# Two of four value products of a head as three rounded products, with the scaling of the probabilities moved to GpSimd

## What is computed

```python
def prompt_latent_attention(q_lat, q_pe, ckv, kpe):
    ...
    def block(args):
        ql_b, qp_b, i = args
        sc = (jnp.einsum('bqhc,bkc->bhqk', ql_b, ckv)
              + jnp.einsum('bqhr,bkr->bhqk', qp_b, kpe)).astype(jnp.float32) * SOFTMAX_SCALE
        sc = jnp.where(kpos[None, :] <= qpos[:, None], sc, -jnp.inf)
        p = jax.nn.softmax(sc, axis=-1).astype(ckv.dtype)
        return jnp.einsum('bhqk,bkc->bqhc', p, ckv)

def mla_output(o_lat, z, w_kv_up, w_out):
    o = jnp.einsum('bthc,chv->bthv', o_lat, w_kv_up[..., QK_NOPE_DIM:]).reshape(b, t, D_ATTN)
    return (o * jax.nn.silu(z)) @ w_out
```

## Time and profile before

| | |
|---|---|
| median of 3 runs | 2006.69 us (2005.28 to 2007.47) |
| the profiled execution | 2006.08 us, of which the span of its instructions 2004.4 us |
| TensorE busy | 1945.2 us, 97% of the span |
| VectorE, ScalarE, GpSimd busy | 1415.9 us (71%), 848.7 us (42%), 171.9 us (9%) |
| second group of heads | 1454.7 to 1519.3 us, 64.6 us |
| its end, from the first product of `scores(1)` on | 1492.87 to 1519.3 us |

### The profile page before, as it was taken

The page is one execution under the profiler, slowest core; times in us unless marked ns, Lnnn a source line. Parts: engine busy times, 40 slices in busy tenths (PEclk is TensorE's granted clock), DMA queues, the critical chain, the costliest instruction groups (busy, mean ns, idle before and its releaser), DMA issues.

```text
span 2004.4 us, 42248 instructions
## 1 busy us (share of the span) xinstructions
PE 1945.2 (97%) x16142; PEld 1831.3 (91%) x16142; DVE 1415.9 (71%) x2073; ACT 848.7 (42%) x1318; POOL 171.9 (9%) x124
## 2 busy tenths in 40 slices
PE   4999999999999999999999999999999999999997
PEld 3899999999999999999999999999888887779996
DVE  5597777777777777798778996667433456669776
ACT  3243333333333333364455644446543444455443
POOL 1200000000000000000000250003221122200002
PEclk9999999999999999999999999999999999999998
DMA  9976555555555556654554434448422239852447
GB/s 392 405 268 215 201 196 194 194 194 194 196 203 203 198 203 205 223 190 150 157 181 171 160 131 140 136 134 314 134 72 84 84 104 348 289 184 97 138 149 285
DMA packets 134902, 386.69 MB, mean 193 GB/s; under 512 B 13906, under 2 KB 44498, under 8 KB 131858
## 3 DMA queue, kind: packets, MB, share of 16 engines
q1 hardware_dynamic: 129682, 368.52, 53.2%
q0 software_dynamic: 5120, 16.78, 2.7%
HBM read 353.92 MB, written 31.33 MB: 192 GB/s over the span
## 4 chain that ended last, share of the span: by engine, by line
PE 81%; DVE 8%; DMA 6%; issue 2%; ACT 1%; SPq 1%; DVEq 0%; ACTq 0%
PE ps L965 36%; PE ps L969 18%; DMA s<-adastream 4%; PE ps L912 3%; PE ps L1441 3%; PE ps L846 3%; PE ps L1324 2%; PE ps L1291 2%; PE ps L1306 2%; PE ps L1467 2%; PE ps L1381 2%; DVE w_split L2176 1%; PE ps L898 1%; PE ps L853 1%; DMA w_raw<-wstream 1%
## 5 line engine op out<-in xcount | busy, mean ns | idle before, releaser
L1623 ACT ACTIVATE w_split<-w_raw 128x1024 fp32r<-128x1024 f32 x204 | 216.0, 1059 | 380.4 <-PE ps L969 206.7
L2176 DVE TENSOR_TENSOR w_split<-w_raw,w_split 128x1024 fp32r<-128x1024 f32 x212 | 259.5, 1224 | 139.5 <-ACT w_split L1623 134.6
L965 PE MATMUL ps<-operand_hi,w_split 128*128 128x288 f32 x1224 | 328.5, 295 | 0.0
L965 PE MATMUL ps<-operand_lo,w_split 128*128 128x288 f32 x1224 | 328.3, 294 | 0.0
L965 PE MATMUL ps<-t_hi,w_split 128*128 128x288 f32 x960 | 262.9, 300 | 0.9 <-ACT w_split L1623 0.7
L965 PE MATMUL ps<-t_lo,w_split 128*128 128x288 f32 x960 | 258.0, 295 | 0.0
L790 POOL TENSOR_TENSOR w_split<-w_raw,w_split 128x1024 fp32r<-128x1024 f32 x47 | 126.0, 2681 | 1499.2 <-ACT w_split L1561 1499.2
L965 PEld LDWEIGHTS ps<-operand_hi,w_split 128*128 128x128 f32 x1224 | 229.8, 188 | 0.1
L965 PEld LDWEIGHTS ps<-operand_lo,w_split 128*128 128x128 f32 x1224 | 229.7, 188 | 0.0
L965 PEld LDWEIGHTS ps<-t_hi,w_split 128*128 128x128 f32 x960 | 180.3, 188 | 10.3 <-issue 8.9
L969 PE MATMUL ps<-operand_hi,w_split 128*128 128x288 f32 x1224 | 186.8, 294 | 0.1
(11 more groups left out here) (409 smaller groups left out, 3876.7 us busy)
## 6 DMA issues: line engine op xcount, KB each, us to landing
w_raw<-wstream SPq DMA_DIRECT2D x169, 512.0 KB, 3.6
ada_ring<-adastream SPq DMA_DIRECT2D x112, 512.0 KB, 4.8
a<-wstream SPq DMA_DIRECT2D x88, 512.0 KB, 4.7
s<-wstream SPq DMA_DIRECT2D x44, 512.0 KB, 3.4
ada_first_ring<-adastream SPq DMA_DIRECT2D x32, 512.0 KB, 9.3
ada_third<-adastream SPq DMA_DIRECT2D x32, 512.0 KB, 6.5
tiles<-y_park SPq DMA_DIRECT2D x12, 1152.0 KB, 7.6
x_residual<-x_in SPq DMA_DIRECT2D x8, 1152.0 KB, 8.7
```

The source lines that it names most:

```text
L965: pe.matmul(PS[:, bank, 0:HALF], WH[:, c.slot, k * P:(k + 1) * P], x(k), start=(first and k == 0 and x is hi), stop=False, skip_group_chec ...
L1623: act.activation(WH[:, c.slot, :], raw, ACT.Copy).then_inc(w_hi_ready, 1)
L2176: dve.tensor_tensor(WL[:, c.slot, :], raw, WH[:, c.slot, :].bitcast(F32), ALU.subtract).then_inc(w_lo_ready, 1)
```

## The change

The value products of the key tiles 0 and 1 are made of three rounded products each: high values by high probabilities, high values by low probabilities, low values by high probabilities. Tiles 2 and 3 stay as they are. For this the high parts are what ScalarE copies out of PSUM (`PTH`, `VH`), and VectorE subtracts them from what is still in PSUM: `values_low` once a group (four subtractions of 256 columns) and `probs_low(j)` for each head (512 and 384 columns), into places of their own (`PTL`, `VL`). `turn_probs(0)` waits for the values' low parts, `turn_probs(j)` and `values(j)` for those of the probabilities. GpSimd scales the probabilities, in an order written out around its six weight chunks, once VectorE has made the reciprocals of the first three rows and then of the last (`row_factors`). VectorE's list in a group is interleaved anew. The four semaphores of the loaded key weights become one.

```diff
@@ gpsimd
+            def normalise(g, j):
+                for i in range(QT):
+                    if i in (0, 3):
+                        pool.wait_ge(sums_turned, g * 2 * G + (2 * j + 1 + i // 3))
+                    o, w = P * (i * (i + 1) // 2), (i + 1) * P
+                    pr = PROBS[j % 2][:, o:o + w]
+                    last = pool.tensor_scalar(pr, pr, MX[:, 12 + i:13 + i], None, ALU.mult)
+                last.then_inc(p_ready, 1)
+
             pool.wait_ge(w_lo_ready, W_ROPE)
-            with pool.Fori(0, (W_OUT - W_ROPE) // 2 + 1) as i:
-                rest(Chunk(W_ROPE, 2, i))
-                rest(Chunk(W_ROPE + 1, 2, i))
+            for n in range(W_ROPE, W_GRP + 2):
+                rest(Chunk(n))
+            for g in range(H // G):
+                n = Chunk(W_GRP + 2 + 6 * g)
+                for c in range(4):
+                    rest(n + c)
+                normalise(g, 0)
+                for c in range(4, 6):
+                    rest(n + c)
+                for j in range(1, G):
+                    normalise(g, j)
@@ tensor
-                    pe.wait_ge(wk_landed[j], g * 16 + 16)
+                    pe.wait_ge(wk_landed, g * 64 + 64)
@@ turn_probs
                     if j == 0:
                         pe.wait_ge(v_evac, g * G + G)
+                        pe.wait_ge(v_lo, g * 2 + 2)
                     else:
                         pe.wait_ge(pt_evac, g * 12 + 3 * j)
+                        pe.wait_ge(p_lo, g * G + j)
@@ values
                     pe.wait_ge(o_done, g * G + (j + BEGUN))
+                    pe.wait_ge(p_lo, g * G + (j + 1))
...
-                        w = QT - k
-                        last = pe.matmul(PS[:, 7, k * P:TP], V[:, k, j * VD:(j + 1) * VD], PT[:, s * P:(s + w) * P],
-                                         start=(k == 0), stop=(k == QT - 1))
-                        s += w
+                        c = slice(s * P, (s + QT - k) * P)
+                        v = slice(j * VD, (j + 1) * VD)
+                        if k < 2:
+                            low = VL[k][j // 2][:, j % 2 * VD:(j % 2 + 1) * VD]
+                            terms = ((VH[:, k, v], PTH[:, c]), (VH[:, k, v], PTL[k][:, :]), (low, PTH[:, c]))
+                        else:
+                            terms = ((V[:, k, v], PT[:, c]),)
+                        for i, (value, prob) in enumerate(terms):
+                            last = pe.matmul(PS[:, 7, k * P:TP], value, prob, start=(k == 0 and i == 0), stop=(k == QT - 1))
+                        s += QT - k
@@ evac
-                        act.activation(PT[:, 4 * c * P:4 * c * P + w], PS[:, 4 + c, 0:w], ACT.Copy).then_inc(pt_evac, 1)
+                        high = (w, 3 * P, 0)[c]
+                        if high:
+                            last = act.activation(PTH[:, 4 * c * P:4 * c * P + high], PS[:, 4 + c, 0:high], ACT.Copy)
+                        if high < w:
+                            last = act.activation(PT[:, 4 * c * P + high:4 * c * P + w], PS[:, 4 + c, high:w], ACT.Copy)
+                        last.then_inc(pt_evac, 1)
...
-                    act.activation(V[:, t, :], PS[:, 4 + t, :], ACT.Copy).then_inc(v_evac, 1)
+                    act.activation((VH if t < 2 else V)[:, t, :], PS[:, 4 + t, :], ACT.Copy).then_inc(v_evac, 1)
@@ vector
+            dve.wait_ge(stored, 32)
             step(copy(QPS[:, :, :, :], QPE_EARLY[:, :, :, :]))
@@ group
-                def maxima(j):
+                def maxima(j, rows=range(QT)):
...
-                def normalise(j):
-                    dve.wait_ge(exp_done, g * 16 + (4 * j + 4))
-                    step(dve.reciprocal(MX[:, 12:16], MX[:, 8:12]))
-                    for i in range(QT):
-                        o, w = P * (i * (i + 1) // 2), (i + 1) * P
-                        pr = PROBS[j % 2][:, o:o + w]
-                        last = dve.tensor_scalar(pr, pr, MX[:, 12 + i:13 + i], None, ALU.mult)
-                    last.then_inc(p_ready, 1)
+                def row_factors(j):
+                    if j:
+                        dve.wait_ge(p_ready, g * G + j)
+                    for rows in (slice(0, 3), slice(3, 4)):
+                        dve.wait_ge(exp_done, g * 16 + (4 * j + rows.stop))
+                        dve.reciprocal(MX[:, 12 + rows.start:12 + rows.stop], MX[:, 8 + rows.start:8 + rows.stop]).then_inc(sums_turned, 1)
+
+                def values_low():
+                    for k in range(2):
+                        dve.wait_ge(v_evac, g * G + (k + 1))
+                        for i in range(2):
+                            c = slice(2 * i * VD, 2 * (i + 1) * VD)
+                            last = dve.tensor_tensor(VL[k][i][:, :], PS[:, 4 + k, c], VH[:, k, c].bitcast(F32), ALU.subtract)
+                        last.then_inc(v_lo, 1)
+
+                def probs_low(j):
+                    dve.wait_ge(pv_done, g * G + (j + BEGUN))
+                    for c, w in enumerate((4 * P, 3 * P)):
+                        dve.wait_ge(pt_evac, g * 12 + (3 * j + c + 1))
+                        o = slice(4 * c * P, 4 * c * P + w)
+                        last = dve.tensor_tensor(PTL[c][:, :], PS[:, 4 + c, 0:w], PTH[:, o].bitcast(F32), ALU.subtract)
+                    last.then_inc(p_lo, 1)
...
-                for j in range(G):
-                    maxima(j)
-                    normalise(j)
-                    if j >= 2:
-                        out(j - 2)
+                maxima(0)
+                row_factors(0)
+                maxima(1, range(0, 2))
+                values_low()
+                maxima(1, range(2, QT))
+                row_factors(1)
+                maxima(2, range(0, 2))
+                probs_low(0)
+                maxima(2, range(2, QT))
+                row_factors(2)
+                maxima(3, range(0, 2))
+                out(0)
+                probs_low(1)
+                maxima(3, range(2, QT))
+                row_factors(3)
+                out(1)
+                probs_low(2)
                 sample_query(0)
                 sample_query(1)
                 out(2)
+                probs_low(3)
```

More of the change, by code:

```diff
@@ L236, in build @@
         AT = at("mod_scale", place(KT * NM), [P, KT, NM])
-        CST = at("conv_state", place(KT * 18), [P, KT * 18])
+        co_at = place(KT * 18)
+        CST = at("conv_state", co_at, [P, KT * 18])
         TURN = at("ada_turned", place(AT4 * RG), [P, AT4, RG])
@@ L261, in build @@
         PROBS = [at(f"probs{i}", ro + 10 * P * i, [P, 10 * P]) for i in range(2)]
+        PTH = at("probs_t_hi", xo, [P, 7 * P], F32R)
+        PTL = [at("probs_t_lo0", ao + 2 * T + CT * T, [P, 4 * P], F32R), at("probs_t_lo1", ro + 20 * P, [P, 3 * P], F32R)]
+        VH = at("values_hi", po + 10496, [P, 2, G * VD], F32R)
+        VL = [[at(f"values_lo{k}{i}", o, [P, 2 * VD], F32R) for i, o in enumerate(places)]
+              for k, places in enumerate(((xo + 4352, po + 14080), (co_at, mo + CT * P)))]
         PRS = at("probs_sample", to, [P, PAST])
@@ L415, in build @@
         q_hi, q_lo, k_hi, k_lo = sem("q_hi"), sem("q_lo"), sem("k_hi"), sem("k_lo")
-        wk_landed = [sem(f"wk_landed{i}") for i in range(G)]
+        wk_landed, v_lo, p_lo, sums_turned = sem("wk_landed"), sem("v_lo"), sem("p_lo"), sem("sums_turned")
         v_evac = sem("v_evac")
@@ L687, in load_wk @@
             def load_wk(h, s):
-                sp.dma_start(WK[s][:, :], wk_in[bass.ds(h, 1), :, :].rearrange("a p n -> p (a n)")).then_inc(wk_landed[s], 16)
+                sp.dma_start(WK[s][:, :], wk_in[bass.ds(h, 1), :, :].rearrange("a p n -> p (a n)")).then_inc(wk_landed, 16)
             def load_rope(g, turns, s):
@@ L2742, in _ @@
             dve.wait_ge(rope_hi, 3 * (H // G))
+            dve.wait_ge(stored, 32)
             step(copy(QPS[:, :, :, :], QPE_EARLY[:, :, :, :]))
             def group(g, last=False):
-                def maxima(j):
-                    for i in range(QT):
+                def maxima(j, rows=range(QT)):
+                    for i in rows:
                         dve.wait_ge(score_done, g * 16 + (4 * j + i + 1))
@@ L2892, in sample_first @@
                 sample_prepare(0, QS_FIRST)
-            loop(0, H // G - 1, G * (QT + 1), group)
+            loop(0, H // G - 1, G * QT, group)
             group(H // G - 1, last=True)
```

## The result

The changed kernel takes 2010.53 us (median of 18 runs, 2009.36 to 2014.62) where the kernel before takes 2006.89 (median of 18 runs beside them): ratio 1.0022, 95% interval 1.0016 to 1.0029. It is slower by 0.22%, 4.4 us by the ratio and 3.6 by the medians: little, but clear of the noise. The forecast was +2.4 us, no difference that can be told as the likeliest case, and slower by over 0.2% with a chance of 0.31; the measured ratio stands right at that border.

The account below looks back on a forecast made before the run. TensorE, busy 97% of the span, was taken to bound the kernel. Per group -1.14 + 0.25 + 0.80 + 0.70 = +0.6 us, four groups +2.4 us, gave 2009.1 us, range 2003.5 to 2013.5.

Parts of the forecast that it names:

- The gain, 0.285 us a head: In `values(j)`, rounded products in place of full-precision ones for two key tiles: 1.14 us saved a group, 4.55 in the run.
- (a): At `turn_probs(0)`, head 0's transposes wait for VectorE's subtractions of the values: 0.25 us more a group.
- (b): At `values(0)`, TensorE stands from 1500.75 to 1501.54 for VectorE's probability remainders: 0.8 us lost a group.
- (c): At `values(1)`, TensorE waits from 1507.7 to 1508.42 for remainders behind head 3's rows and `out(0)`: 0.7 us lost a group.
- TensorE starts 0.12 to 0.14 us after what it stalls on: Restart delay of TensorE after any stall, used in the hand-worked order at a group's end: 0.12 to 0.14 us.
- (d): At `values(2)` and `values(3)`, behind the sample queries, remainders end 0.4 us or more before TensorE arrives: no loss.
- GpSimd, 2.4 us a head, between 1.3 and 3.4: GpSimd's scaling of a head's four rows: 2.4 us taken, lower bound VectorE's 1.27, upper 3.4 from two-input subtractions.
- the decision point: GpSimd's scaling time from which it would delay TensorE's transposes of heads 1 and 3: about 4.8 us a head.
- that rival: GpSimd is the bound: at 6 us a head its scaling delays transposes of heads 1 and 3, 2017.8 us; chance 10%.
- The remainders come out in time: Rival: VectorE's remainders cause TensorE no waits, leaving the whole gain of 4.55 us, 2002.1 us; in time or nearly, 10%.

Follow-up runs that it names:

- the last two variants of the remainders-last order: Changed kernel, remainders last and `turn_probs(0)` wait split, VectorE scaling each head's last row: 2005.07 us; also `out(0)` before `maxima(3)`'s first two rows: 2005.31 us.

## Why the prediction came out as it did

The mechanism was right and the sum too small: +0.6 us a group forecast, +1.0 measured, in the four groups of heads. The term that was mis-sized is the restart of TensorE behind a wait at the value products, and an error the other way at the transposes hid 0.10 us a group of it, which is luck.

- *The gain, 0.285 us a head.* 0.28 measured, by the distance of the transposes of heads 2 and 3. The rounded products start 0.23 and 0.18 us apart as the rows of before had it. The 216 and 162 ns of the Trainium skill (TensorE: Matmul & The Clock Gate, Back-to-back issue gap) do not agree with this trace either; the section gives them for a product by itself, and for a sustained stream some 131 ns at 512 columns, which is further off.
- *(a), +0.25 us at the transposes of head 0.* 0.15. The four subtractions take 1.41 us, as forecast (1.45); the transposes start 0.06 us after they end, where the forecast took 0.12.
- *(b), 0.8 lost at values(0), and (c), 0.7 at values(1).* 1.04 and 0.92, from the distance of the transposes (7.24 us between those of heads 0 and 1, where it was 6.48, plus the gain of 0.28; 7.07 where it was 6.43). VectorE is not the cause: its remainders of head 0 end at 1505.15, and by hand, with the 3.75 us by which the group's end began later in this profile, it was 1501.42 + 3.75 = 1505.17. Those of head 1 end 0.17 us later than by hand (1512.22 to 1512.05), but TensorE arrives there 0.17 later as well. The step that was too small is "TensorE starts 0.12 to 0.14 us after what it stalls on". At the value products it is 0.24 us (1505.15 to 1505.39), since the wait for ScalarE's copy, long met, and the working out of its count stand behind that wait in TensorE's list; the run with the waits in another order took 0.10 of it away. And the first product after it holds the engine for 0.33 us instead of 0.23 (1505.39 to 1505.72). So `values(0)` takes 1.96 us in place of the 1.87 to 1.9 forecast. Twice a group 0.12 + 0.10 are 0.44, less 0.10 for (a): 0.34 of the 0.4 us by which a group is over the forecast. That what stands behind the wait costs 0.10 is shown by the run that took it away. The 0.10 of the first product is read from the traces: where nothing stalls in front of it at heads 0 and 1, in the run with the remainders last, it holds the engine for 0.24 and 0.23 us (1500.35 to 1500.59, 1506.56 to 1506.79). But at heads 2 and 3, behind the sample queries, it takes 0.31 in the changed kernel with no wait recorded, so a stall is not the only thing that lengthens it, and why it is longer is not shown.
- *(d), no wait at heads 2 and 3.* Right; it needs GpSimd to have the scaling, as the run with the scaling back on VectorE shows, where `values(2)` waits too.
- *GpSimd, 2.4 us a head, between 1.3 and 3.4.* 4.26: outside the bounds. The reason for the upper one, that one input costs no more than two, is false here. It cost nothing since the decision point was worked out at 4.8 us; with a chance of 10% for that rival the margin was thinner than it looked. It was also stated too wide: 4.8 us is 1.4 times the two-input price of 3.4 us, not 1.6 times. In the run with the remainders last it is used up.
- *The remainders come out in time* is not what happened, but the 2002.1 us given for it are what TensorE's work takes: 2001.99 us without them.

The change fails by its order and not by its arithmetic. Six of the eight value products moved in front of the wait for VectorE's signal turn +4.4 us into -3.0.

## What to carry to other kernels

When an engine at 97% is to wait for a new operand, put first in its list whatever does not need that operand: here 1.4 us of products were at hand, and the wait was 0.9. Price a stall as the lateness of the signal plus getting going again, which was 0.06 us at the transposes and 0.24 plus 0.10 at the value products here, and leave nothing behind the last wait. After that look for the next engine in the row: once a wait is covered, work moved between or within the helpers may only shift where the main engine stands, as in the last two variants of the remainders-last order (64.22 and 64.24 us a group, where that order alone has 63.98).

## What the runs showed of the hardware

- GpSimd's scaling of float32 in SBUF costs 603, 923, 1243 and 1563 ns for 128, 256, 384 and 512 columns: 2.5 ns a column and 0.28 us fixed. That is more than its subtraction of two inputs (2.2 ns a column and 0.13 fixed by the earlier trace rows) and 3.3 times VectorE's 0.48 us for 512 in the kernel before. The Trainium skill (GPSIMD Engine Reference, Engine selection) has one-input work at roughly line rate; the trace does not agree, with the constant factor (1492 ns for 512) no more than with one for each row.
- The granted clock fell, for some 3 us at a time, in single executions. Behind one pause of TensorE ahead of the groups it did so in two of twelve profiles, the changed kernel's and that of the scaling alone, to means of 0.59 to 0.84 over stretches of 3 us, so in part to the lower level of 1.2 GHz. A late transfer had lengthened the pause to 1.76 us in both, and the fall cost 1.45 us (48 query products in 8.13 us instead of 6.68). The kernel before kept 1.00 there after a pause of 0.92 us, and the run with the remainders last after 1.49. Nine of the twelve profiles have such a stretch around 1053 us, in an earlier stage, and the profile of before has none. The length of the pause alone does not decide it: the run with the scaling back on VectorE waits 2.01 us in its first group (the product at 1438.39) and 2.01 in its second, and the clock fell in the first alone, in the second it stayed at 1.00:

```profile
1437.00:1440.00 3.00, 1.61 (x5) 1.39 (x6) 2.81 (x7) 1.32 (x5) 0.00 (x0) 0.82 0.02 5
1440.00:1443.00 3.00, 3.00 (x17) 2.81 (x16) 1.45 (x5) 1.07 (x3) 0.00 (x0) 0.61 0.00 0
```

In the groups of the changed kernel, whose waits are 0.7 to 0.9 us, the clock stayed at 1.00.
